# Conditioning rows amid the levels of the even mixer, rotary part by pairs of heads, and the order of its masks and differences

## The reference

```python
def modulate_2(x, shift, scale):
    return x * (1.0 + scale) + shift
# mod_l = silu(c) @ ada_w[l] + ada_b[l]: nine rows of 1024 for each layer ("conditioning")

def gla_chunked(q, k, v, log_g, s0, include_diag):
    # S_t = diag(a_t) S_{t-1} + k_t^T v_t ; o_t = q_t S_t
    def step(s, inp):
        b = jnp.cumsum(gi, axis=-2)
        decay = jnp.exp(jnp.where(mask, b[i] - b[j], -inf))
        att = jnp.einsum('bhid,bhjd,bhijd->bhij', qi, ki, decay)
        o = einsum(att, vi) + einsum(qi * jnp.exp(b), s)
        ...

def apply_rope(x, cos, sin):
    x0, x1 = x[..., 0], x[..., 1]          # neighbouring pairs
    out = stack([x0 * cos - x1 * sin, x0 * sin + x1 * cos])

def dense_attention(q, k, v, scale):        # in blocks of 128 queries
    p = softmax(einsum('bqhd,bkhd->bhqk', q, k) * scale)
    return einsum('bhqk,bkhd->bqhd', p, v)

def even_mixer(...):
    o = gla_chunked(forward) + flip(gla_chunked(backward))
    gla = rms_norm(o, norm_g) * silu(r)
    q = concat(q_nope, apply_rope(q_rope)); k = concat(k_nope, apply_rope(k_rope))
    mla = dense_attention(q, k, v)
    return concat(gla, mla) @ w_out
```

## Time and profile before

| | |
|---|---|
| median of 3 runs | 3272.02 us (3270.83 to 3273.89) |
| profiled execution, own time | 3275.61 us |
| its span | 3273.7 us |
| instructions | 45787 |
| granted TensorE clock, mean | 0.951 |
| HBM read over the span | 533.30 MB, 163 GB/s |

### The profile page before, as it was taken

The page is one execution under the profiler, slowest core; times in us unless marked ns, Lnnn a source line. Parts: engine busy times, 40 slices in busy tenths (PEclk is TensorE's granted clock), DMA queues, the critical chain, the costliest instruction groups (busy, mean ns, idle before and its releaser), DMA issues.

```text
span 3273.7 us, 45787 instructions
## 1 busy us (share of the span) xinstructions
PE 3034.9 (93%) x19910; PEld 2351.9 (72%) x19910; DVE 1376.1 (42%) x2090; ACT 1073.4 (33%) x1580; POOL 240.5 (7%) x275
## 2 busy tenths in 40 slices
PE   6988899889999989999988888999989999898998
PEld 4866699845555548888677646888868887774898
DVE  4655555532222233333476354333343333436554
ACT  4443354322222233222432233222242222435443
POOL 0014470200000000000004000000000000200000
PEclk9988899879999989999899898999999999898999
DMA  7557756389999943232339221333222323310453
GB/s 230 157 183 227 251 156 180 131 331 392 389 395 389 396 177 113 81 109 72 109 117 322 66 69 58 103 93 103 82 88 80 106 86 105 130 65 1 142 185 100
DMA packets 415174, 537.41 MB, mean 164 GB/s; under 512 B 14292, under 2 KB 389876, under 8 KB 390260
## 3 DMA queue, kind: packets, MB, share of 16 engines
q1 hardware_dynamic: 414964, 534.38, 47.9%
HBM read 533.30 MB, written 1.05 MB: 163 GB/s over the span
## 4 chain that ended last, share of the span: by engine, by line
PE 82%; DVE 8%; ACT 5%; DMA 3%; issue 1%; POOL 0%; DVEq 0%; SPq 0%; ACTq 0%
PE ps L189 80%; DVE ar L244 2%; PE ps L188 2%; ACT ar L314 2%; DMA RAW<-in_ada_w 1%; DVE LR L244 1%; ACT HR L314 1%; DMA RAW<-in_w_ada 1%; DMA RAW<-in_w_in 1%; DVE ar L260 1%; DVE ar L250 1%; DVE ar L263 1%; ACT arf1i L314 1%; PE ps L195 1%; ACT L314 1%
## 5 line engine op out<-in xcount | busy, mean ns | idle before, releaser
L189 PE MATMUL ps<-AH,HR 128*128 128x512 f32 (+1 forms) x2488 | 877.1, 353 | 38.6 <-DVE AL L244 17.0
L189 PE MATMUL ps<-AL,HR 128*128 128x512 f32 (+1 forms) x2488 | 868.6, 349 | 0.0
L189 PE MATMUL ps<-AH,LR 128*128 128x512 f32 (+1 forms) x2488 | 867.8, 349 | 0.0
L244 DVE TENSOR_TENSOR LR<-RAW,HR 128x2048 fp32r<-128x2048 f32 (+3 forms) x232 | 485.9, 2095 | 601.7 <-ACT HR L314 596.2
L314 ACT ACTIVATE HR<-RAW 128x2048 fp32r<-128x2048 f32 (+3 forms) x232 | 404.4, 1744 | 709.8 <-PE ps L189 632.6
L189 PEld LDWEIGHTS ps<-AH,HR 128*128 128x128 f32 x2488 | 477.7, 192 | 109.1 <-ACT ar L314 18.7
L189 PEld LDWEIGHTS ps<-AH,LR 128*128 128x128 f32 x2488 | 477.8, 192 | 59.0
L189 PEld LDWEIGHTS ps<-AL,HR 128*128 128x128 f32 x2488 | 478.2, 192 | 57.1
L189 PE MATMUL ps<-ar 64*128 64x128 f32 (+9 forms) x1318 | 239.6, 376 | 36.8 <-DVE ar L244 18.8
L244 POOL TENSOR_TENSOR ar<-ar 128x384 f32<-128x384 f32 (+5 forms) x138 | 151.0, 1102 | 1295.5 <-DMA ar<-in_cst 1024.4
L189 PEld LDWEIGHTS ps<-ar 64*128 64x128 f32 (+2 forms) x1318 | 142.1, 192 | 118.1 <-issue 47.0
(11 more groups left out here) (195 smaller groups left out, 3656.4 us busy)
## 6 DMA issues: line engine op xcount, KB each, us to landing
RAW<-in_ada_w SPq DMA_DIRECT2D x72, 1024.0 KB, 6.4
RAW<-in_f1i SPq DMA_DIRECT2D x44, 1024.0 KB, 5.1
RAW<-in_f2i SPq DMA_DIRECT2D x44, 1024.0 KB, 5.1
RAW<-in_w_in SPq DMA_DIRECT2D x32, 1024.0 KB, 5.6
RAW<-in_w_ada SPq DMA_DIRECT2D x24, 1024.0 KB, 8.6
RAW<-in_w_eu SPq DMA_DIRECT2D x17, 1024.0 KB, 9.5
HF<-in_w_ed SPq DMA_DIRECT2D x17, 1024.0 KB, 8.4
LF<-in_w_eu SPq DMA_DIRECT2D x17, 1024.0 KB, 10.1
```

What stands on the lines that cost most here:

```text
L189: return self.e.matmul(o, w, x, start=start, stop=stop)
L244: return self.e.tensor_tensor(o, a, b, op) if self.e else NOTHING
```

## The change

1. `conditioning_act` copies the row first and takes the tile (with its look-ahead) after it, in every stage.
2. `Engine` has a flag `ahead`. Inside the levels ACT and DVE pass row tiles with `past()`, which cuts nothing. After level 10 the flag is set again, and in level 12 both engines cut the next two tiles of the plan (the two of cq).
3. A level has one conditioning step of PE between the two halves of its pairs and one behind them, levels 12 and 13 none. So the levels hold 24 rows instead of 28; the steps of the softmax loop are moved from turn 0 on to turns 7 and later, and make five rows there (turns 7 to 11).
4. On DVE the difference of level 0 stands ahead of the diagonal products; the product of level n+1 stands between the masked copies of the two halves of level n; the copies no longer wait for each other.
5. The rotary part is done in three pieces (key; heads 0 and 1; heads 2 and 3), the third one inside turn 0 behind the maximum; scores wait only for their own piece. The temporary is `P[2]`.
6. The four lower halves of the linear attention's rows are made in turns 0 to 3, one each.

```diff
@@ class Engine
         self.e, self.K, self.seen, self.jobs, self.at, self.tick = e, K, {}, [], 0, tick
+        self.ahead = True
...
+    def past(self):
+        self.j += 1
@@ def conditioning_act
         c = job.base + s
-        S.take()
         S.wait_ge(*pe.of("row", c))
...
         K.free(act, "row", c)
+        S.take() if S.ahead else S.past()
@@ def conditioning_dve
     if s < job.n:
-        V.take()
+        V.take() if V.ahead else V.past()
@@ class Even
-        self.xs = [self.qr[Q, i, 256:512] for i in range(4)] + [self.krr[Q, 256:512]]
+        self.xs = [self.krr[Q, 256:512].unsqueeze(1)] + [self.qr[Q, i:i + 2, 256:512] for i in (0, 2)]
...
+def level_steps(n):
+    return 1 if n < 12 else 0
@@ def gla_pe
-    def pairs(n, k, q):
+    def pairs(n, k, q, steps=0):
         for tp in range(2):
+            T.step(steps if tp else 0)
             bs = [bank("att", n, p, tp) for p in range(2)]
...
-        pairs(n, o.KQ[n % 2], o.KQ[n % 2])
-        T.step(2)
+        pairs(n, o.KQ[n % 2], o.KQ[n % 2], level_steps(n))
+        T.step(level_steps(n))
@@ def gla_act
+    S.ahead = False
     referred(0)
     for n in range(14):
         if n < 13:
             referred(n + 1)
-        S.step(2)
+        S.step(2 * level_steps(n))
+        S.ahead = n > 10
+        if n == 12:
+            S.cut(S.j + 1)
@@ def gla_dve
+    referred(0)
     V.wait_ge(K.loaded["glam"], 16)
...
-    referred(0)
+    weighted(0)
+    V.ahead = False
     for n, (lv, d) in enumerate(o.levels):
         if n < 13:
             referred(n + 1)
+        V.wait_ge(*dve.of("att"))
...
                 V.wait_ge(*pe.of("att", n, p, tp))
-                V.wait_ge(*dve.last)
                 V.put(o.ATT[p][tp], mk, ...)
...
-        V.step(2)
+            if n < 13 and tp == 0:
+                weighted(n + 1)
+        V.step(2 * level_steps(n))
+        V.ahead = n > 10
+        if n == 12:
+            V.cut(V.j + 1)
@@ def latent_pe
     for i, x in enumerate(o.xs):
-        T.mm(bank("turned rope", i)[Q, 0:256], o.rsw[Q, :], x, True, True).then_inc(*pe("rope", i))
-    T.wait_ge(*dve.of("rope"))
+        c = 256 * x.shape[1]
+        T.mm(bank("turned rope", i)[Q, 0:c]..., o.rsw[Q, :], x, True, True).then_inc(*pe("rope", i))
     for n in range(19):
         if n < 16:
             hd, qt, nk = o.work[n]
+            T.wait_ge(*dve.of("rope", 1 + hd // 2))
...
-        T.step()
+        T.step(1 if n > 6 else 0)
@@ def latent_act
-            S.wait_ge(*dve.of("rope"))
...
-        S.step()
+        S.step(1 if n > 6 else 0)
@@ def latent_dve
-    for i, x in enumerate(o.xs):
...
+    def rope(i):
+        x, c = o.xs[i], o.xs[i].shape[1]
+        t = o.P[2][Q, 0:256 * c]...
+        V.wait_ge(*pe.of("rope", i))
+        V.tt(x, x, cos, MUL).then_inc(*dve())
+        then(V.tt(t, K.ps("turned rope", i)..., sin, MUL))
+        K.free(dve, "turned rope", i)
+        then(V.tt(x, x, t, ADD), "rope", i)
+    rope(0)
+    rope(1)
...
-    for m in range(4):
-        split(m, o.oT[:, m, :])
...
             then(V.ts(mx, mx, -(192.0 ** -0.5), None, MUL), "mmax", n)
-        V.step()
+        if n == 0:
+            rope(2)
+        V.step(1 if n > 6 else 0)
+        if n < 4:
+            split(n, o.oT[:, n, :])
```

More of the change, by code:

```diff
@@ L2666, in gla_dve, with referred, weighted @@
         K.free(dve, "state", n)
+    def referred(n):
+        lv, d = o.levels[n]
+        w = 1 << lv
+        bv, dv = (o.halves(x, w) for x in (o.bs[d], o.KQ[n % 2]))
+        ref = (bv[:, :, 0, w - 1:w] if d == 0 else bv[:, :, 1, 0:1]).broadcast_to([128, 512 // w, w])
+        lo = bv[:, :, 0, :]
+        V.wait_ge(*pe.of("att", n - 2 if n > 1 else -1, 1, 1))
+        if d == 0:
+            V.tt(dv[:, :, 0, :], ref, lo, SUB).then_inc(*dve("referred", n))
+        else:
+            V.tt(dv[:, :, 0, :], lo, ref, SUB).then_inc(*dve("referred", n))
+    def weighted(n):
+        lv, d = o.levels[n]
+        w = 1 << lv
+        dv, kv, qv = (o.halves(x, w) for x in (o.KQ[n % 2], o.kT, o.qT))
+        V.wait_ge(*act.of("kq", n))
+        V.tt(dv[:, :, 0, :], dv[:, :, 0, :], (kv if d == 0 else qv)[:, :, 0, :], MUL).then_inc(*dve("kq", n))
+    referred(0)
     V.wait_ge(K.loaded["glam"], 16)
@@ L2808, in latent_pe @@
     for i, x in enumerate(o.xs):
-        T.mm(bank("turned rope", i)[Q, 0:256], o.rsw[Q, :], x, True, True).then_inc(*pe("rope", i))
-    T.wait_ge(*dve.of("rope"))
+        c = 256 * x.shape[1]
+        T.mm(bank("turned rope", i)[Q, 0:c].rearrange("p (a b) -> p a b", b=256), o.rsw[Q, :], x, True,
+             True).then_inc(*pe("rope", i))
     for n in range(19):
@@ L2924, in latent_dve @@
     V.wait_ge(*act.of("qr"))
-    for i, x in enumerate(o.xs):
+    def rope(i):
+        x, c = o.xs[i], o.xs[i].shape[1]
+        t = o.P[2][Q, 0:256 * c].rearrange("p (a b) -> p a b", b=256)
+        cos, sin = (y[Q].unsqueeze(1).broadcast_to([64, c, 256]) for y in (o.cos, o.sin))
         V.wait_ge(*pe.of("rope", i))
-        V.tt(x, x, o.cos[Q], MUL).then_inc(*dve())
-        then(V.tt(o.P[0][Q, 0:256], K.ps("turned rope", i)[Q, 0:256], o.sin[Q], MUL))
+        V.tt(x, x, cos, MUL).then_inc(*dve())
+        then(V.tt(t, K.ps("turned rope", i)[Q, 0:256 * c].rearrange("p (a b) -> p a b", b=256), sin, MUL))
         K.free(dve, "turned rope", i)
-        then(V.tt(x, x, o.P[0][Q, 0:256], ADD), "rope")
+        then(V.tt(x, x, t, ADD), "rope", i)
+    rope(0)
+    rope(1)
     def split(m, src):
```

## The result

Twenty executions of each kernel on one chip: before 3270.65 us (3262.88 to 3278.24), after 3275.65 us (3272.68 to 3278.76). The ratio is 1.0015, 95% interval 1.0008 to 1.0021: the change costs about 5 us, less than the 0.2% called no change. Forecast were 3264.0 us and a range of 3256 to 3271, so the time came out above the range, on the other side of the kernel before. The 5 us are read from the twenty, the causes from single stages.

What follows compares the result with a forecast made beforehand. TensorE carries 82% of the chain, but VectorE's chain and the DMA end each level. Terms -15.6 + 13.0 - 4.8 - 0.6 = -8.0 us, taken from the median 3272.0, gave 3264.0 us, range 3256 to 3271.

Steps and rivals of the forecast that it cites:

- Levels, -15.6: Linear attention levels: fewer row tiles queue ahead of cq's first tile, so cq starts about 1795.2 instead of 1810.78 us.
- the rival on the slower side: Levels: VectorE and GpSimd operations block each other, 7.0 us per level; +6 us, 3278; chance 0.07.
- Rows and cuts in the loop, +13.0: Softmax loop: five rows and the last small matmul cost 7.3 us, two cuts stall TensorE 5.7; bounds 7.3 to 16.
- The rival by which the cuts cost nothing: Softmax loop: cuts cost TensorE nothing because the copies had slack; about -13.5 us, 3258.5; chance 0.13.
- the walk: Turns 10 to 12 of the softmax loop: 15 to 16 us with cuts against about 9.7 for TensorE alone.
- What the loop gains, -4.8: Start of softmax loop: rotary by pairs brings the first transpose 5.3 us sooner, 4.8 kept; bounds 3 and 6.3.
- Order of row and cut, -0.6: All stages: ScalarE copies the row before the cut; first stage may gain 0.7 us, bounds -1 to +1.
- The cover named: Row copy before cut, all stages: TensorE wants the row only at its next step, one weight tile later.
- the forecast's -8.0: Whole kernel: sum of the four terms, against the profiled 3275.6 us; own range -3.5 to -12, chance 0.58.

Runs made afterwards that it cites:

- e1: Kernel before with only the rotary part and the four low halves in turns 0 to 3; ratio 0.9998, softmax stretch 58.6 us against 61.4.
- e11: Changed kernel with both cuts out of turns 10 and 11 and the look-ahead before the row copy again; ratio 0.9974 to before, stretch 68.4 us.
- e6: Changed kernel with both look-ahead cuts out of turns 10 and 11, the first tile halved in turns 16 and 18; ratio 0.9987 to before, stretch 65.9 us.
- e13: Changed kernel with the first of the loop's five rows in the wait before the first scores, four in turns 7 to 10; ratio 0.9999 to before.
- e3: Changed kernel with the five conditioning rows in turns 0 to 4 instead of 7 to 11; ratio 0.9998 to before, stretch 78.7 us.
- e4: Changed kernel with six extra matmuls, changing no result, in the wait before the first scores; ratio 1.0005 to before, stretch 75.7 us.
- e15: Changed kernel with the rotary part and low halves of before, the five rows still in turns 7 to 11; ratio 1.0035 to before, stretch 79.2 us.
- e10: Changed kernel with old row/cut order, one row in the rotary wait, four between output product tiles, first tile cut during the query product; ratio 0.9969 to before.
- e14: Changed kernel with cuts late, old order of row and cut, and the first of five rows in the rotary wait; ratio 0.9973 to before, stretch 62.4 us.

## Why the prediction was wrong

**Levels, -15.6.** Right in mechanism and nearly in size. Rows every 3.0 us at a DMA share of 1.10 with 21 row tiles ahead of cq, as counted; cq starts 79.5 us after the first pair, where the forecast's 1714.8 and 1795.2 make 80.4. VectorE and GpSimd taking turns (the rival on the slower side) is small: where the two meet, GpSimd's product takes 1.29 us (1.79 before) and VectorE's 0.75 (0.69 before), well inside the 3.0 of a row. By the rule of the Trainium skill, "SBUF — State Buffer", section SBUF: two separate sides, they exclude each other; the longer times agree with it, though the two records overlap by 0.2 us, and it costs nothing here. What was off is the base: the one execution at hand had levels of 94.8 us, three others 92.1 to 92.7. The gain from the first pair on is 12.6 to 13.2 for the usual execution, 15.3 against that one. The forecast's 15.6 also holds an earlier start of the pairs, 1.2 us; it is 0.6 (7.0 us behind the product without decay instead of 7.6). Together 13.2 to 13.8.

**Rows and cuts in the loop, +13.0.** Right in mechanism, 1.5 low in size, and wrongly split. From transposes to transposes the seven turns that hold rows and cuts take 14.5 us more than in e1: 0.7, 1.3, 1.3, 1.3, 3.7, 5.0 and 1.1. In e11, the same rows without the cuts, they take 5.5 more: five rows cost 5.5, not 7.3, and the cuts 9.0, not 5.7. The two stalls are 2.59 and 2.96 us, 5.6 together; the other 3.4 fit half of the 6.8 us at 1.2 GHz that the record has around them. The 5.7 came out right partly by luck: the walk (15 to 16, less 9.7, less 0.6) gives 4.7 to 5.7, so it took the upper end, and it held the tiles to be in time. The first one landed 6.5 us after its issue and kept ScalarE waiting 1.21 us, which passes through VectorE into the first stall. The rival by which the cuts cost nothing falls with e6 and e11.

**What the loop gains, -4.8.** This step failed. The first transposes came 12.8 us after the first rotary matmul, 4.9 sooner than before, as the prediction put it. But it priced the scores at the low clock of the earlier trace rows and then let the clock rise as before. It took the row at the low clock and the cut behind it out of turn 0, never asking how long the low level would last without them. It lasted 20.5 us instead of 10.2. The next three turns ran at 1.2 GHz and took 12.4 us, 5.1 more than in the kernel before: the whole gain was gone by turn 3. That it is the clock e13 shows: with the wait filled and the clock at 2.4 GHz they take 7.7. A further spell over the loop's end, which nothing in the forecast held, cost 2.5 in the stretch and 1.4 in the output product; what starts it isn't shown (e3, e4 and e15 don't have it, e10, e13 and e14 do). The new rotary code alone is worth 2.8 (e1), beside late rows 0.6 (e15).

**Order of row and cut, -0.6.** The gain foreseen in the first stage is there (1.3), and a loss that was not foreseen takes it back: up to +1.5 by the stages, +2 to +5 by the ratios, at or over the bound of +1. The cover named (TensorE wants the row only a step later) holds for the row; the price is at the cut behind it, which comes later.

**The sum.** -13.5 (levels), +17.3 (stretch), +1.4 (start of the output product), about +1 (order): +6, where +5.0 (2.6 to 6.9) was measured. Beside the forecast's -8.0 the base makes about 2 of the difference, the stretch 9.1 (5.1 in the first turns, 1.5 in the seven turns, 2.5 at the loop's end), the start of the output product 1.4 and the order 1.5 or more. Most of it is TensorE's clock: 5 us in the first turns, 3.4 around the stalls, 2.5 at the loop's end, 1.4 behind it; the rows, 1.8 cheaper than forecast, gave some back. No rival named the clock, and the only rival on the slower side was another mechanism.

**What stays open.** What ends a low spell. A wait ahead of the first scores (1.87 us, or 4.8 with the old rotary part) came before the fall in every kernel that had one, and filling it with a row kept the clock up three times of three; extra matmuls in it did so for 10 us only. But the length of the spell was 6.8 to 30.7 us over kernels that start alike, and 10.2 in one (e6) against 20.5 in four with the same first ten turns. And the gain of a filled wait is shown in the stretch (6.8 us in e13, 6.1 in e14), not in the time of the whole kernel: e13's ratio fell as it should, e14's did not.

## What to carry to other kernels

When an edit shortens or moves work around a place where TensorE waits, read the granted clock of the windows there and price the work behind it at both levels; here 20 us at 1.2 GHz ate all that the earlier start won. Look for a wait of one or two microseconds ahead of a long dependent loop and put background work into it: a row that cost 1.3 us in the loop (e11) cost nothing there, and the stretch ran 6.5 us faster up to turn 3. When work that is cut in advance moves with its rows, check that its tile has landed by then. And take the base of a sum from more than one execution, or at least look for a pause in it that needn't return.

## What was not expected of the hardware

TensorE stayed at 1.2 GHz while it was busy: 18.9 of 20 us in after, 29.2 of 30 in e3. Extra matmuls in the wait (e4) moved the fall by 10 us, a conditioning row in the same place (e13) removed it. And spell and stretch repeat between two executions of one kernel (20.5 and 20.5, 10.2 and 10.2; 78.65 and 78.64, 61.39 and 61.38), while the levels of the kernel before differ by 2.1.
